# Borders between sublayers in two token parts, the last output unit's squares summed by TensorE, and all values projected feature by feature

## The reference

```python
def ffn_sublayer(h, m, sub, g_pre, g_post, w1, w2):
    shift, scale, gate = mods_of(m, sub)
    y = swiglu(modulate(rms_norm(h, g_pre[sub]), shift, scale), w1, w2)
    return h + 0.5 * gate * rms_norm(y, g_post[sub])
# mixer: h = modulate(rms_norm(x, g_pre[1]), sh, sc); q, k, v, fu = split(h @ w_in)
#   o = concat(neighbourhood attention, window attention, fourier_mix(fu)) @ w_out
#   x = x + gt * rms_norm(o, g_post[1])
# the last layer (odd): u = rmsnorm(h); q, k, v, g = split(u @ w_in, 4); ... h + o @ w_out
```

## Time and profile before

| | us |
|---|---|
| median of 3 runs | 4057.22 (4055.41 to 4086.95) |
| profiled execution, its time | 4081.47 |
| its span | 4079.7 |
| TensorE busy in it | 3769.8 (92%) |
| VectorE, ScalarE, GpSimd busy | 1781.7, 1187.7, 1033.1 |
| mean granted TensorE clock | 0.939 |

### The profile page before, as it was taken

How to read it: one execution, slowest core, us unless ns; L and a number is a source line. 1 busy time by engine, 2 the same in 40 slices (tenths; PEclk the granted TensorE clock), 3 DMA queues, 4 the chain that set the end, 5 groups by cost and what they waited for, 6 DMA issues and landing times.

```text
span 4079.7 us, 56053 instructions
## 1 busy us (share of the span) xinstructions
PE 3769.8 (92%) x21621; PEld 3201.2 (78%) x21621; DVE 1781.7 (44%) x2394; ACT 1187.7 (29%) x1745; POOL 1033.1 (25%) x419
## 2 busy tenths in 40 slices
PE   5999998978899999899999897889998999879998
PEld 4888887856788888788888785778878898678655
DVE  6564454167435332535353615642246463521134
ACT  3212122146231212331212313532234423211352
POOL 1332331200123232223232130124441232123201
PEclk9999997989799999799999798989998998889898
DMA  5333332110123222123232131013331121012101
GB/s 183 125 128 129 103 108 70 52 38 6 47 80 115 92 95 88 57 82 114 93 113 88 47 101 43 30 63 95 96 108 62 57 79 56 24 45 83 57 1 52
DMA packets 88273, 316.62 MB, mean 78 GB/s; under 512 B 10432, under 2 KB 11712, under 8 KB 87488
## 3 DMA queue, kind: packets, MB, share of 16 engines
q1 hardware_dynamic: 85056, 300.21, 23.0%
q10 hardware_dynamic: 3072, 14.40, 1.0%
HBM read 312.48 MB, written 2.10 MB: 77 GB/s over the span
## 4 chain that ended last, share of the span: by engine, by line
issue 73%; POOL 18%; PE 9%; POOLq 0%; DVE 0%; ACT 0%; ACTq 0%
POOL w_parts L468 18%; PE psum L1475 4%; PE psum L1832 1%; PE psum L1816 1%; PE psum L1855 1%; PE psum L1841 1%; PE psum L1820 0%; POOLq L467 0%; POOLq L472 0%; PE psum L1834 0%; DVE final L1390 0%; DVE final L1391 0%; DVE sq_sum L1316 0%; POOLq L468 0%; PE psum L1822 0%
## 5 line engine op out<-in xcount | busy, mean ns | idle before, releaser
L1475 PE MATMUL psum<-h_parts,w_parts 128*128 128x512 f32 (+2 forms) x12192 | 2159.0, 340 | 81.8 <-DVE h_parts L887 41.8
L1475 PEld LDWEIGHTS psum<-h_parts,w_parts 128*128 128x128 f32 x12192 | 1880.9, 191 | 356.7 <-issue 57.1
L468 POOL TENSOR_TENSOR w_parts<-w_raw,w_parts 128x1024 fp32r<-128x1024 f32 x415 | 1032.9, 2490 | 3029.7 <-ACT w_parts L490 3029.7
L490 ACT ACTIVATE w_parts<-w_raw 128x1024 fp32r<-128x1024 f32 x415 | 439.7, 1061 | 2200.1 <-PE psum L1475 2035.6
L1475 PE MATMUL psum<-hidden_parts,w_parts 128*128 128x512 f32 x3696 | 678.4, 346 | 0.8 <-DVE hidden_parts L862 0.8
L1475 PEld LDWEIGHTS psum<-hidden_parts,w_parts 128*128 128x128 f32 x3696 | 583.7, 188 | 93.5 <-DVE hidden_parts L862 1.3
L966 DVE TENSOR_TENSOR to_split<-silu_gate,psum 128x768 f32<-128x768 f32 (+1 forms) x88 | 78.1, 888 | 769.9 <-PE psum L1475 769.9
L931 DVE SCALAR_TENSOR_TENSOR mod_ring<-mod_ring,cond_rows 128x1024 f32<-128x1024 f32 x128 | 252.4, 1972 | 0.0
L862 DVE TENSOR_TENSOR hidden_parts<-to_split,hidden_parts 128x768 f32 (+1 forms) x88 | 184.8, 2100 | 101.3 <-ACT hidden_parts L495 101.3
L929 DVE SCALAR_TENSOR_TENSOR mod_products<-mod_ring,cond_rows 128x1024 bf16<-128x1024 f32 x128 | 165.1, 1290 | 18.8 <-DMA mod_ring<-modw_dram 17.4
L1438 PE MATMUL psum<-const,squares 128*128 128x1 f32 x624 | 132.6, 348 | 39.7 <-ACT squares L504 39.7
(11 more groups left out here) (270 smaller groups left out, 2615.1 us busy)
## 6 DMA issues: line engine op xcount, KB each, us to landing
w_raw<-wu_dram SPq DMA_DIRECT2D x415, 512.0 KB, 3.5
mod_ring<-modw_dram SPq DMA_DIRECT2D x128, 512.0 KB, 4.2
mod_first<-modw_dram SPq DMA_DIRECT2D x16, 512.0 KB, 5.6
na_bias<-rpb_dram ACTq DMA_DIRECT2D x6, 896.0 KB, 4.7
four_dft<-four_dram ACTq DMA_DIRECT2D x2, 2048.0 KB, 8.0
resid<-xT_dram SPq DMA_DIRECT2D x1, 2048.0 KB, 12.9
out_dram<-final SPq DMA_DIRECT2D x8, 256.0 KB, 2.0
cond_rows<-condb_dram SPq DMA_DIRECT2D x1, 1024.0 KB, 5.2
```

Of the source, the lines that this page charges most:

```text
L468: pool.tensor_tensor(SPL[:, s % 2, 1], RAW[:, s % 2], SPL[:, s % 2, 0].bitcast(F32), ALU.subtract).then_inc(w_split, 1)
L490: act.activation(SPL[:, u % 2, 0], RAW[:, u % 2], ACT.Copy).then_inc(w_hi, 1)
L1475: ins = pe.matmul(PS[:, pair, PSO[a]:PSO[a] + z - a], SPL[:, s, wp, k], src[:, xp, k, t0 + a:t0 + z], start=k == 0 and n_ == 0, stop=k == ...
```

## The change

**Borders.** The tokens are cut into two parts (`HALVES`): 512 and 256 where there are 768, 256 and 256 where there are 512. `post`, the entry squares, sums, root, reciprocal, row spreading and `pre` go part by part, each with semaphores of its own. The residual squares get eight buffers of their own (`SQE`, in the hidden activations' space), so they no longer wait for TensorE. Lists are interleaved by hand: TensorE spreads the rows of part 0 between tiles 1 and 2 of part 1's sums, and those of part 1 after k = 4 of the first units; ScalarE and VectorE take root and reciprocal at fixed places. The first two units of a sublayer (`first_pair`) are computed together on part 0, k by k; on part 1 unit 0 goes k by k and unit 1 after it. A mixer's unit 2 waits for all 16 pieces of `pre`. SP's weight and modulation loads wait for the rows of part 0 where they waited for the rows of all tokens.

**Last output unit.** With 768 tokens, unit 7 is computed span by span (512, then 256) and signals after the first. `ACC` takes only seven units' squares; those of the last are summed by TensorE straight from `SQ`, in the same accumulation. `sub["post"]` has two parts, one in the last sublayer.

**Values.** `token_units` and the padding of the 528-token activations go. All six value units of a mixer and all eight of the last layer are feature-major units, with copies, transposes (six or four per mixer unit, five in the last layer) and a second copy.

The core of the diff (indentation shortened, blank lines left out):

```diff
...
+SQE = place("entry_squares", [P, DT, T1], F32, a_arena + 20480)
...
     d = t - MOD_FIRST
-    sp.wait_ge(rb_ready, subs[idx]["in"]["q"] + 1)
...
+def entry_root(sub, hi):
...
+    a, z = sub["halves"][hi]
+    act.wait_ge(esum_ready, sub["in"]["eh"] + hi + 1)
+    act.activation(ST[:, 1, a // P:z // P], PS[:, 2, SEQ * hi:SEQ * hi + (z - a) // P], ACT.Sqrt, scale=1.0 / D,
+                   bias=col("eps")).then_inc(eroot_ready, 1)
...
+def entry_squares(sub, before=None):
...
+    for hi, (a, z) in enumerate(sub["halves"]):
+        for m in range(DT):
+            if before is not None:
+                act.wait_ge(resid_ready, before["xr"] + 8 * hi + m + 1)
+            act.activation(SQE[:, m, a:z], XT[:, m, META + a:META + z], ACT.Square).then_inc(esq_ready, 1)
+            if hi == 1 and m == 3:
+                entry_root(sub, 0)
...
+def pre_apply(sub, e0):
...
+            if hi == 0 and k == 3:
+                entry_root(sub, 1)
...
+    act.wait_ge(sq_added, sq + DT - 2)
+    for hi, (a, z) in enumerate(sub["post"]):
+        act.wait_ge(last_y, sub["in"]["ph"] + hi + 1)
+        act.activation(SQ[:, 1, a:z], Y[:, DT - 1, a:z], ACT.Square).then_inc(last_sq, 1)
+    act.wait_ge(unit_done, u + DT)
+    high_part(u, 0, DT + 1)
+    for hi, (a, z) in enumerate(sub["post"]):
+        act.wait_ge(ysum_ready, sub["in"]["ph"] + hi + 1)
+        act.activation(ST[:, 1, a // P:z // P], PS[:, 2, SEQ * hi:SEQ * hi + (z - a) // P], ACT.Sqrt, scale=1.0 / D,
+                       bias=col("eps")).then_inc(yroot_ready, 1)
...
-    act.wait_ge(v_split, b["e"] + 8)
+    act.wait_ge(v_split, b["e"] + 16)
...
+def entry_recip(sub, hi):
...
+    a, z = sub["halves"][hi]
+    dve.wait_ge(eroot_ready, sub["in"]["eh"] + hi + 1)
+    dve.reciprocal(ST[:, 2, a // P:z // P], ST[:, 1, a // P:z // P]).then_inc(erec_ready, 1)
...
+def pre(sub, b):
...
+    for i, (hi, a, z, k) in enumerate(tiles):
+        if k == 0:
+            dve.wait_ge(erow_ready, b["eh"] + hi + 1)
+        v_free(e + i)
+        dve.scalar_tensor_tensor(V[:, k % 2, a:z], XT[:, k, META + a:META + z], mod_col(l, 3 * s + 1, k, int(a >= SEQ)),
+                                 PS[:, 2, SEQ * hi:SEQ * hi + z - a], ALU.mult, ALU.mult).then_inc(v_ready, 1)
+        if i > 0:
+            low(i - 1)
+        if hi == 0 and k == 4:
+            entry_recip(sub, 1)
+    low(15)
...
+def post(sub, b, after):
...
+    for hi, (a, z) in enumerate(sub["post"]):
+        dve.wait_ge(yrow_ready, b["ph"] + hi + 1)
+        for m in range(DT):
+            step(dve.tensor_tensor(Y[:, m, a:z], Y[:, m, a:z], PS[:, 3, SEQ * hi:SEQ * hi + z - a], ALU.mult))
+            dve.scalar_tensor_tensor(XT[:, m, META + a:META + z], Y[:, m, a:z], mod_col(l, 3 * s + 2, m, int(a >= SEQ)),
+                                     XT[:, m, META + a:META + z], ALU.mult, ALU.add).then_inc(resid_ready, 1)
+            if after is not None and hi == 1 and m == 5:
+                entry_recip(after, 0)
...
+        if hi == 0 and T == T1:
+            dve.wait_ge(last_half, ph // 2 + 1)
+        else:
+            dve.wait_ge(unit_done, u + DT)
+        if first:
+            dve.tensor_copy(Y[:, m, a:z], PS[:, 3, a:z]).then_inc(last_y, 1)
+        else:
+            dve.tensor_tensor(Y[:, m, a:z], Y[:, m, a:z], PS[:, 3, a:z], ALU.add).then_inc(last_y, 1)
+    dve.memset(PRM[:, 15:16], 0.0).then_inc(psum_read, 1)
...
+        if j < 16:
+            value_features(j)
+        if j > 10:
+            value_rows(j - 1)
...
-        dve.wait_ge(unit_done, u + j + 2)
-        t = token_psum(u + j, 5)
-        c = (j - 1) * P
-        dve.tensor_copy(VV[:, 0:4, c:c + 2 * P], t[:, 0:4])
-        dve.tensor_copy(VV[0:META, 4, c:c + 2 * P], t[0:META, 4]).then_inc(psum_read, 2)
+    def value_features(j):
+        dve.wait_ge(unit_done, u + j + 1)
+        if j >= 3:
...
     rows(q, un + 3, T)
...
+def entry_rows(sub, hi):
+    a, z = sub["halves"][hi]
+    pe.wait_ge(erec_ready, sub["in"]["eh"] + hi + 1)
+    for o in range(a, z, P):
+        ins = pe.matmul(PS[:, 2, SEQ * hi + o - a:SEQ * hi + o - a + P], ST[:, 2, o // P:o // P + 1].broadcast_to([P, P]),
...
+    ins.then_inc(erow_ready, 1)
...
+def entry_stats(sub):
+    for hi, (a, z) in enumerate(sub["halves"]):
+        for m in range(DT):
+            if hi == 1 and m == 2:
+                entry_rows(sub, 0)
+            pe.wait_ge(esq_ready, 8 * sub["in"]["eh"] + 8 * hi + m + 1)
+            for j, o in enumerate(range(a, z, P)):
+                ins = pe.matmul(PS[:, 2, SEQ * hi + j:SEQ * hi + j + 1], SQE[:, m, o:o + P], col("ones"),
+                                start=m == 0 and j == 0, stop=m == DT - 1, skip_group_check=True)
...
+    b = sub["in"]
+    u, e, T = b["u"], b["e"], sub["T"]
+    pe.wait_ge(w_split, u + 2)
+    for semaphore, value in waits:
+        pe.wait_ge(semaphore, value)
+    def column(j, k, a, z):
+        for n_, (wp, xp) in enumerate(((0, 0), (0, 1), (1, 0))):
+            ins = pe.matmul(PS[:, (u + j) % 4, a:z], SPL[:, (u + j) % 2, wp, k], H[:, xp, k, a:z],
+                            start=k == 0 and n_ == 0, stop=k == DT - 1 and n_ == 2)
+        return ins
+    halves = [(a, z) for a, z in sub["halves"] if a < T]
+    for hi, (a, z) in enumerate(halves):
...
+        done = hi == len(halves) - 1
+        for k in range(DT):
+            pe.wait_ge(v_split, e + 8 * hi + k + 1)
+            ins = column(0, k, a, z)
+            if done and k == DT - 1:
+                ins.then_inc(unit_done, 1)
+            if hi == 0:
+                ins = column(1, k, a, z)
+                if k == 4:
+                    entry_rows(sub, 1)
+        if hi == 1:
+            for k in range(DT):
+                ins = column(1, k, a, z)
+    ins.then_inc(unit_done, 1)
 def unit(u, i, j, src, T, KT, wait, ready=None, cap=DT, t0=0):
...
+                                start=k == 0 and n_ == 0, stop=k == KT - 1 and n_ == 2)
+        ins.then_inc(unit_done if z == T else last_half, 1)
+    pe.wait_ge(sq_added, sq + DT - 1)
+    for hi, (a, z) in enumerate(sub["post"]):
+        for j, o in enumerate(range(a, z, P)):
+            pe.matmul(PS[:, 2, SEQ * hi + j:SEQ * hi + j + 1], ACC[:, o:o + P], col("ones"), start=j == 0, stop=False,
+                      skip_group_check=True)
+    for hi, (a, z) in enumerate(sub["post"]):
+        pe.wait_ge(last_sq, ph + hi + 1)
+        for j, o in enumerate(range(a, z, P)):
+            ins = pe.matmul(PS[:, 2, SEQ * hi + j:SEQ * hi + j + 1], SQ[:, 1, o:o + P], col("ones"), start=False, stop=True,
+                            skip_group_check=True)
+        ins.then_inc(ysum_ready, 1)
+    for hi, (a, z) in enumerate(sub["post"]):
+        pe.wait_ge(yrec_ready, ph + hi + 1)
+        for o in range(a, z, P):
+            ins = pe.matmul(PS[:, 3, SEQ * hi + o - a:SEQ * hi + o - a + P], ST[:, 2, o // P:o // P + 1].broadcast_to([P, P]),
+                            col("ident", 0, P), start=True, stop=True)
+        ins.then_inc(yrow_ready, 1)
 def out_units(u, pr, src, T, KT, entry, ready, cap=DT):
     with pe.Fori(0, 2) as i:
...
+        pe.wait_ge(vf_ready, 6 * mx + j - 9)
+        for t in range((T1 if j < 14 else T) // P):
             ins = pe.transpose(PS[:, (u + j) % 4, t * P:t * P + P], V[:, j % 2, t * P:t * P + P], col("ident", 0, P))
...
-    pe.wait_ge(psum_read, pr + 10)
-    tiles = [(t * P, t * P) for t in range(6)]
-    token_units(u + 13, H[:].rearrange("p a k t -> p (a k t)"), tiles, n=1)
-    value_rows(12)
-    pe.wait_ge(psum_read, pr + 12)
-    token_units(u + 14, H[:].rearrange("p a k t -> p (a k t)"), tiles[0:T // P])
+    value_rows(15)
     pe.wait_ge(psum_read, pr + 16)
...
+        for t, (a, z) in enumerate(SSD_TILES):
+            ins = pe.transpose(PS[0:z - a, (u + j) % 4, t * P:t * P + P], V2[:, j % 2, a:z], col("ident", 0, P))
+        ins.then_inc(sv_rows, 1)
+    for j in range(1, 12):
...
```

291 lines of the change are left out of this document (156 added, 135 removed).

## The result

The changed kernel takes **3967.7 us** (median of 4 runs, 3959.3 to 3969.5) against 4072.0 for the kernel before beside it (4 runs, 4055.4 to 4087.0): ratio 0.9741, 95% interval 0.9709 to 0.9774. The forecast was 3960, range 3930 to 3995. The profiled executions took 3966.3 and 4081.5; their spans, 3964.5 and 4079.7, differ by 115.2 us.

The account below looks back on a forecast made before the run. TensorE, busy 92% of the span, bounds the kernel, so time comes off its waits or shortened work. Values 61.6 plus borders 43.3 less 7 for the clock is 98, scaled to 97: 4057.2 - 97 = 3960 us, range 3930 to 3995.

Parts of the forecast that it names:

- Step 1: Borders of 768 tokens: the last output unit, computed span by span, costs 0.35 us more.
- Step 2: Border: `ACC` no longer takes the last square, so `post` begins 5.7 us after the last unit instead of 10.2.
- Step 3: Border, `post` and part 0's sums: TensorE sets the pace, and `pre` begins at 25.5 us instead of 37.5.
- Step 4: Border, after six more tiles' sums: first products at 30.7 us, half clock about 6 us, part 0 ends at 45.
- Step 5: Border, new wait: part 1 of `pre` needs rows spread at 41.0 us; last piece 49.5, unit 0 ends 50.0.
- Step 6: Border, second new wait, for unit 2's weights: ready at 54.9 us into a feed-forward, 55.3 into a mixer.
- The clock: Part 1 of the borders: at a fallen clock unit 1's tail costs 15 us over five places; half taken, 7.
- (a): Borders give next to nothing: 256-token pieces cost what 512 cost, and the clock falls; 3995; chance 0.14 together with (c).
- (b): The clock stays high in the borders' sums: 20 us more gained, 3940; chance 0.12.
- (c): Value units are paced by copies or weights: 25 us gained instead of 62, 3996; chance 0.14 together with (a).
- (d): Borders: VectorE does all `post` before `pre`, only sums overlap; `pre` at 31, 3980; chance 0.68 shared with the forecast.
- (e): First units after each border stay at the half clock, so the kernel is slower, 4159; chance 0.03.

Follow-up runs that it names:

- the halved sums: The changed kernel with only the even tiles' squares summed by TensorE at each sublayer's entry (result not the reference's): 3946.3 us, ratio 0.9682.
- the yardstick: The changed kernel run again, unchanged, beside the follow-up runs: 3957.2 us, ratio 0.9711; in a later group 3960.7 us, ratio 0.9728.
- with TensorE full: The changed kernel with added products, their results discarded, to keep TensorE busy in the borders: 3978.0 us, ratio 0.9759.

## Why the prediction was right, and where not

**Values.** 61.6 forecast, 63.7 measured: 29.8 for 30.0, 23.1 for 23.4 in the mixers, 50.4 for 52.0 in the last layer, from the end of unit 0 to unit 9 (6.39 a unit; the first two have no transposes between them). The copies behind unit 15 show as forecast, 29.8 - 3 x 9.12 = 2.4, and no unit waits for weights.

**Step 1**, the last unit span by span for 0.35 us: wrong and tiny. 36 instructions took 6.46, as 36 of the 252 before them, 44.68 / 7 = 6.38. **Step 2**: `post` at 6.0, forecast 5.7; undoing it costs 3 us a border. **Step 3**: `pre` at 25.6, forecast 25.5, paced by TensorE; the halved sums show the pace. **Step 4**: first products at 30.4 (30.7), part 0 done at 672.07 + 6.02 - 633.1 = 45.0 (45). **Step 5**: the new wait is there, rows of part 1 at 38.6 (41.0), last piece 47.3 (49.5), VectorE idle 2.25. VectorE starts on them at 39.2. They came sooner because the half clock ended within the first five k: 5 us at 0.67 are some 3 us of it, where step 4 had 6. **Step 6**: unit 2 at 54.1 (55.3), with ScalarE's table DMAs ahead of its weights; border 3 54.2, after 10.7 us of idleness (55.3, and 10).

**The border sum** was too low: 43.3 less 7 for the clock is 36, with 1 for the start in it; measured are 47.5 less the start's 2.4, 45 with the clock in it. The borders 0 to 3 gained 2.0, 1.1, 0.3 and 2.4 us more than their sums before the clock's term, from steps 5 and 6; the other 7 is that term.

**The clock.** Its term was 7 of at most 15. The 30 instructions behind the last piece of unit 0 take 4.15 at the full clock; in the first profile they took 4.15, 5.64 and 5.41 at the borders 0 to 2, and at border 4 36 of them took 8.04, some 3 over the full pace. That is about 6 in all, and about 4 in the yardstick's. So the tail did run at a lower clock, as forecast, but its price was wrong: at the borders into a feed-forward it doesn't reach unit 2. At border 1 the last 24 products took 4.17 us in the first profile and 3.03 in the yardstick's, and unit 2 started 5.1 and 5.0 us after unit 0's end, for TensorE then waited 1.06 or 2.13 us for the weights in any case. The forecast's own step 6 had that wait and didn't set it against the term. (Where the weights were made early, at border 0 of that run, the longer tail does end last.)

**The step that has no line** failed too: that work behind the change, unchanged itself, keeps its time. The value groups' waits had left the half clock on for the first mixer's rotary products and the last layer's projections, and had let GpSimd's two low parts fall beside VectorE's rotary work in the second mixer; some 6 us went with them. The stages behind the values gave 13.2 in these two profiles, but the rest is pace and the opening of the last attention, which no run ties to the change. I had read the clock only at borders, and counted it only as a possible loss.

**From the profile to the median.** Between the profiles the gain is 115, not 98: 2 more from the values, 12 from the borders (7 of them the clock's term), 13 behind the values and 1 of remnants, less 3 at the start and 8 of pace. The median of before was 4057.2 in the runs shown and 4069.5 to 4076.3 over the eleven runs of it beside each later group, so 3960 lies nearer to the result (3967.7, then 3957.2 and 3960.7) than its gain of 97 does: two errors, 7 us in the gain by the medians (17 by the profiles) and 12 to 19 in the yardstick, stood against each other. The mechanism of the borders and the values was right; that the time came out within 8 us of 3960 is in part luck.

**Rivals.** (a) fell: 256-token pieces run at their 0.85 and 0.98, and the borders gave 47.5. (b) fell: the clock is 0.50 through the sums, even with TensorE full. (c) fell. (d): the sums alone overlap, as it says, and that was in the forecast; its 31 for `pre` fell. (e) fell: 1.00 from 668 on at border 0, and where the tail ran lower, the units behind it did not stay there.

## What to carry to other kernels

Splitting a serial chain in two token parts moved the wait instead of ending it: after such a change look for the instruction that the second part waits for, and where it stands in its engine's order; moving two issues and one wait (rows after k = 2, weights ahead of table DMAs, the second mixer's wait for all pieces behind unit 2) gave 17 us more by the traces, 24 by the medians. One-column sums are cheap to count and dear at the half clock; having fewer of them beats giving them company. When waits on TensorE go, credit the dense work behind them too, if the rows show it starting at the half clock, and stop crediting where they show the full clock again.

## What the runs showed of the hardware

Dense units of the same code run at two paces at a granted clock of 1.00: 199.68 or 203.52 us for the first 24 units of a feed-forward sublayer, 1.9% apart, constant within a sublayer and different between executions. A sublayer of 768 tokens is 8 us shorter at the faster (3.84 there, 169.60 or 166.40 in the next part, 1 in the last output units). All three sublayers at one or the other would be 24 us of the 36 between the fastest and the slowest run of the kernel before (4055.0 to 4091.1). What chooses the pace was not tried and stays open.

A VectorE addition of 512 columns from SBUF took 2.72 us instead of 0.69 beside GpSimd's low parts, in two profiles of the kernel before; the one beside it with an input in PSUM kept its 0.69.
